# Low parts of weights by another VectorE instruction, and one in four of them by GpSimd in 56 units of the second table

## The reference

```
u   = peer_u[expert]                  # 128 rows per token, gathered
act = gelu(h . u)                     # one number per token and expert
y   = sum(gate * act * peer_v[expert])
out = layer_norm(alpha * h + y)
```

## Time and profile before

| what | us |
|---|---|
| median of three runs | 3760.6 |
| the profiled execution | 3774.7 |
| its span, first to last instruction | 3772.9 |
| first table, all 64 units, in the span | about 2265 to 3022 |
| second table, all 64 units, in the span | about 3022 to 3757 |

### The profile page before, as it was taken

How to read it: one execution, slowest core, us unless ns; L and a number is a source line. 1 busy time by engine, 2 the same in 40 slices (tenths; PEclk the granted TensorE clock), 3 DMA queues, 4 the chain that set the end, 5 groups by cost and what they waited for, 6 DMA issues and landing times.

```text
span 3772.9 us, 56020 instructions
## 1 busy us (share of the span) xinstructions
PE 3714.0 (98%) x22023; PEld 3316.4 (88%) x22023; DVE 2759.2 (73%) x3457; ACT 1404.1 (37%) x2037; POOL 1117.6 (30%) x579
## 2 busy tenths in 40 slices
PE   9999999999999999999999999999999999999998
PEld 8888888888987888888888899999999987878787
DVE  5655566565788765556556788899998877898888
ACT  5644444444335100000000144566664443434343
POOL 0000000001645433434444272332332223344342
PEclk9999999999999999999999999999999999999999
DMA  5345555554689999999999759999999999999996
GB/s 194 123 168 188 181 187 189 182 186 179 238 346 421 421 422 411 404 395 402 392 409 385 303 225 384 396 390 389 392 404 407 401 352 383 398 380 399 379 406 256
DMA packets 196692, 1232.58 MB, mean 327 GB/s; under 512 B 20336, under 2 KB 37312, under 8 KB 54976
## 3 DMA queue, kind: packets, MB, share of 16 engines
q1 hardware_dynamic: 110720, 656.51, 45.4%
q0 software_dynamic: 73728, 536.90, 34.8%
q10 hardware_dynamic: 12096, 37.23, 2.5%
HBM read 1193.34 MB, written 36.70 MB: 326 GB/s over the span
## 4 chain that ended last, share of the span: by engine, by line
PE 94%; DMA 3%; DVE 2%; issue 0%; ACT 0%; SPq 0%; DVEq 0%; ACTq 0%
PE dense_ps L1063 26%; PE dense_ps L1066 11%; PE dense_ps L1048 9%; PE dense_ps L1049 9%; PE dense_ps L1050 9%; PE dense_ps L1323 7%; PE dense_ps L1068 5%; PE score_ps L1323 4%; PE dense_ps L1096 3%; DMA wbuf<-in_peer_v_dram 2%; PE o_ps L1323 2%; PE oT_ps L1323 2%; PE dense_ps L1102 2%; PE score_ps L1285 2%; PE score_ps L1175 1%; PE oT_ps L1215 1%
## 5 line engine op out<-in xcount | busy, mean ns | idle before, releaser
L1448 DVE TENSOR_TENSOR w_three<-wbuf,w_three 128x1024 fp32r<-128x1024 f32 x792 | 961.4, 1222 | 457.4 <-ACT w_three L637 455.5
L637 ACT ACTIVATE w_three<-wbuf 128x1024 fp32r<-128x1024 f32 x848 | 890.8, 1059 | 1027.5 <-DMA wbuf<-in_peer_v_dram 235.7
L1048 PE MATMUL dense_ps<-act_two,w_three 128*128 128x256 f32 x2752 | 787.4, 286 | 3.9 <-DVE w_three L1448 3.7
L1049 PE MATMUL dense_ps<-act_two,w_three 128*128 128x256 f32 x2752 | 779.5, 283 | 0.0
L1050 PE MATMUL dense_ps<-act_two,w_three 128*128 128x256 f32 x2752 | 779.5, 283 | 0.0
L1063 PE MATMUL dense_ps<-xT,wbuf 128*128 128x256 f32 x3136 | 688.0, 380 | 0.0
L583 POOL DMA_INDIRECT row<-in_peer_v_dram,expert x203 | 424.5, 2091 | 855.1 <-DVE h L1400 820.1
L1063 PEld LDWEIGHTS dense_ps<-xT,wbuf 128*128 128x128 f32 x3136 | 593.9, 190 | 91.0 <-issue 11.4
L583 POOL DMA_INDIRECT row<-in_peer_u_dram,expert x256 | 449.3, 1755 | 586.8 <-DVE row L1395 526.2
L1395 DVE SCALAR_TENSOR_TENSOR row<-row,h 128x2048 f32<-128x2048 f32 x256 | 573.6, 2286 | 52.8 <-DMA row<-in_peer_u_dram,expert 52.7
L1048 PEld LDWEIGHTS dense_ps<-act_two,w_three 128*128 128x128 f32 x2752 | 529.1, 192 | 15.8 <-issue 11.8
(11 more groups left out here) (293 smaller groups left out, 4324.1 us busy)
## 6 DMA issues: line engine op xcount, KB each, us to landing
wbuf<-in_w_units_dram SPq DMA_DIRECT2D x456, 1024.0 KB
wbuf<-in_peer_v_dram SPq DMA_DIRECT2D x126, 1024.0 KB
gate_spill<-gbuf ACTq DMA_DIRECT2D x8, 2048.0 KB
e_gate<-gate_spill SPq DMA_DIRECT2D x32, 512.0 KB
act_spill<-stage ACTq DMA_DIRECT2D x60, 256.0 KB, 9.0
e_act<-act_spill SPq DMA_DIRECT2D x30, 512.0 KB
row<-in_peer_u_dram,expert POOLq DMA_INDIRECT x256
row<-in_peer_v_dram,expert POOLq DMA_INDIRECT x203, 10.9
```

What stands on the lines that cost most here:

```text
L637: act.activation(hi_of(n)[j // 2][:, j % 2, :], w_of(n)[j // 2][:, j % 2, :], ACT.Copy).then_inc(w_hi_ready, 1)
L1048: nc.tensor.matmul(out, w[0], x[0], start=opens, stop=False)
L1049: nc.tensor.matmul(out, w[0], x[1], start=False, stop=False)
L1448: V.tensor_tensor(lo_of(n)[j // 2][:, j % 2, :], w_of(n)[j // 2][:, j % 2, :], hi_of(n)[j // 2][:, j % 2, :].bitcast(F32), ALU.subtract).t ...
```

## The change

Three edits. (1) by_pool gives quarter 1 of units N_V+4 to N_V+59 (56 units) to GpSimd. (2) GpSimd's program for the second table goes unit by unit: for unit n it issues all gathers whose FREE is at most ROWS_TO[n-2], and then makes the low part of quarter 1 of unit n. (3) VectorE's low parts, in all units, are made by scalar_tensor_tensor (weight * 1.0 - high part) in place of tensor_tensor.

```diff
 def by_pool(n, j):
-    return U_PQ < n < UNITS or UNITS + U_PQ + PLAIN_Q <= n < N_U + 4
+    return U_PQ < n < UNITS or UNITS + U_PQ + PLAIN_Q <= n < N_U + 4 or j == 1 and N_V + 4 <= n < N_V + 60
...
-            def low(n):
-
-                for j in range(4):
+            def low(n, quarters=range(4)):
+
+                for j in quarters:
                     pool.wait_ge(w_hi_ready, HI[n, j])
...
-            for g in range(ROWS_TO[N_U + 1] + 3, LATE_ROWS):
-                gather(g)
-            pool.wait_ge(dense_ready, N_V)
-            for g in range(LATE_ROWS, ALL_ROWS):
+            g = ROWS_TO[N_U + 1] + 3
+            for n in range(N_V + 4, N_V + 62):
+                while g < ALL_ROWS and FREE[g] <= ROWS_TO[n - 2]:
+                    if g == LATE_ROWS:
+                        pool.wait_ge(dense_ready, N_V)
+                    gather(g)
+                    g += 1
+                if n < N_V + 60:
+                    low(n, (1,))
+            for g in range(g, ALL_ROWS):
                 gather(g)
...
                 dve.wait_ge(w_hi_ready, HI[n, j])
-                V.tensor_tensor(lo_of(n)[j // 2][:, j % 2, :], w_of(n)[j // 2][:, j % 2, :], hi_of(n)[j // 2][:, j % 2, :].bitcast(F32), ALU.subtract
-                                ).then_inc(lo_by_dve, 1)
+                V.scalar_tensor_tensor(out=lo_of(n)[j // 2][:, j % 2, :], in0=w_of(n)[j // 2][:, j % 2, :], scalar=1.0,
+                                       in1=hi_of(n)[j // 2][:, j % 2, :].bitcast(F32), op0=ALU.mult, op1=ALU.subtract
+                                       ).then_inc(lo_by_dve, 1)
```

## The result

The changed kernel takes 4045.8 us, the median of four runs (4035.7 to 4046.9), against 3760.0 before (four runs, 3755.3 to 3769.9): 1.076 times as long, with a 95% interval of 1.073 to 1.078. The profiled execution has a span of 4045.1 us, 272.2 more than before.

A forecast was written before the change was run, and what follows sets the result against it. TensorE, busy 98% of the span, was taken as the bound. Units of 17.5 us (15.2 plus 2.3 of clock) against 11.4, over 55 units, gave +336 on 3760.6: 4097 us, range 3950 to 4200.

The forecast's parts named there:

- the forecast's own case: Second table: GpSimd's late low part with the clock falling in each unit, 16.3 to 18.7 us per unit, 4030 to 4162; chance 0.67.
- The other form of the low part costs 0: VectorE's low parts in all units: scalar_tensor_tensor takes the same 1219 ns for 1024 elements as tensor_tensor, so 0 change.
- The row of 2283 ns: Trace row of VectorE's new instruction form at 2048 elements, against 2287 for tensor_tensor; taken as showing equal price.
- The chain of 9.2 us: Second table, from TensorE's third quarter through section n-2's last row, gather and GpSimd's low part: 9.2 us against 5.44 wanted.
- GpSimd and VectorE meet: GpSimd's low part and VectorE's next quarter 0 tie at 6.7 us; 14.6 or 15.8 us per unit, middle 15.2 taken.
- The clock: TensorE restarts at half clock after each unit's wait, losing 2.3 us per unit in quarters 1 and 2; bounds 0 and 2.9.
- 55 units: Units N_V+5 to N_V+59 are bound by the late low part, TensorE waiting for GpSimd some 55 times at 4 to 5 us.
- VectorE's low parts would stay at 1.22 us: In the profile after, VectorE's low parts keep 1.22 us; a change in their length would show the prediction wrong.
- The rival "faster": GpSimd's low part is in time and 64 us off VectorE win back waits: at most 35 us, 3726; chance 0.04.

The follow-up runs named there:

- 3833: The changed kernel, but the last gather before GpSimd's quarter 1 is one row earlier, so it waits for section n-2's last row but one; 3833.0 us, 1.0191.
- 3840: The changed kernel with quarter 3 of the same 56 units on GpSimd in place of quarter 1, same queue order and wait; 3839.7 us, 1.0215.
- 4271: The changed kernel with GpSimd's low part of the second table made twice, one after the other; 4271.5 us, 1.1362.
- the first experiment: The changed kernel, but GpSimd waits only for rows up to section n-3 before making quarter 1 of unit n; 3784.2 us, 1.0064.
- the ninth: The changed kernel with all low parts on VectorE; GpSimd instead subtracts 2 x 512 unused elements per unit, gathers a section earlier; 3787.5 us, 1.0077.
- the last experiment: The changed kernel with the same wait for section n-2's last row, but the gather that followed it issued behind GpSimd's low part; 3937.4 us, 1.0477.
- TensorE kept busy: The changed kernel with 12 further matmuls of 512 columns behind quarter 0 of each of the 56 units; 3969.8 us, 1.0552.

## Why the prediction was right, and where its terms were off

The time was forecast at 4097 and measured at 4046, inside the range and inside the forecast's own case; the change was forecast at +336 us and is +286. Point by point:

- *The other form of the low part costs 0.* Shown: 0.9998 with it alone. The row of 2283 ns was the right one to go by. The Trainium skill's rule on this instruction (Vector Engine (DVE) Microarchitecture Reference, "Points that are easy to get wrong") does not hold for these operands here: 1218 ns against 1219 at 1024 elements.
- *The chain of 9.2 us.* Shown: 9.16 us in the rows above, and by five runs that each change one thing in it: what it waits for (3784 and 3833), when its result is wanted (3840), one link more (4271), one link less (3937). The wait named was the one that ended last.
- *GpSimd and VectorE meet.* The prediction could not tell who comes first and took the middle, 15.2 us per unit. GpSimd gets in: VectorE's low part is recorded from 3512.56, GpSimd's from 3512.59, and it is VectorE's that takes 3.47 us. The chain is then 14.73 us; this term was 0.5 too high. The gather, of which the last 0.9 us run up to 3512.57, lies across VectorE's start and may be what holds it; that was not tried by itself.
- *The clock.* Forecast 2.3 us per unit, the mean of two restarts after 5.07 and 7.14 us. Measured 16.51 - 14.73 = 1.8, of which 0.1 is the mean wait of 3.67 us against the 3.55 of a plain unit: the clock itself is 1.7, as TensorE's 93 us of added busy time over 55 units are too. The waits are shorter than the two that the term was read from, and 9 of 55 units have no low clock at all. This term was 0.5 to 0.6 too high. The two terms together, about 1.0 us times 55, are the 51 us between forecast and result. That they came so close is in part luck: one was the middle of a tie, the other the mean of two restarts whose costs lay 1.25 us apart.
- *55 units.* 55 waits. They are 3.67 us on average where 4 to 5 was written, and so the stage is 1008 us for 1070, its clock 0.89 for 0.85 and its DMA share 0.73 for 0.65.
- *Failed: VectorE's low parts would stay at 1.22 us.* The prediction counted only GpSimd being held up by VectorE, and had named a change in the length of these low parts as a sign of its being wrong. In the changed kernel the median is 1.23 but the mean 1.81 us, as GpSimd holds one of them in most units. In the change this hides, for VectorE stands still for 321 us before its low parts anyway. With the chain removed some 26 us are left (3784), mostly nine waits for GpSimd low parts that were themselves held up.
- *The rival "faster"* rested on 64 us taken off VectorE. It did not come with GpSimd in time in 47 of 56 units either, in the first experiment: GpSimd lengthened VectorE's other instructions by 93 us and took 64 us off it, and TensorE's waits for VectorE went only from 12.9 to 10.7 us. In the ninth, 32 us were lost with no result of GpSimd's on the path.

None of the eleven versions is faster than the kernel before. What remained open: how far a GpSimd low part placed where VectorE runs no instruction with two inputs would help; it was not tried. Not every unit of this order can have such a place of 2.4 us, as VectorE stands still for only 1.7 us of a unit on average ((735 - 627) / 64).

## What to carry to other kernels

When work is moved to an engine with a long idle time, write down what stands in front of it in that engine's queue and what that waits for: here an idle engine delivered 3.7 us late on average in each of 55 units because of a gather's wait, a single gather ahead of the moved work cost 2 us per unit, and one section less of waiting gave back 262 of 286 us. Then look at whether the helper holds up the engine it is to relieve. A short wait of TensorE in every unit can cost more than its length: here 1.7 us per unit of lower clock came on top of 3.7 us of waiting.

## What was not expected of the hardware

- A GpSimd instruction with two SBUF inputs and VectorE's instructions with two SBUF inputs run one after the other, either way round: VectorE's of 1.22 us took up to 3.48 (in the changed kernel), GpSimd's of 2.35 up to 4.82 (in the first experiment). Work that nobody waits for slowed VectorE in the same way. The Trainium skill, SBUF — State Buffer, "Who interferes with whom", states that a VectorE instruction with two SBUF inputs contends with a GpSimd instruction that reads SBUF, and that the order of issue decides who waits. The timeline of the last experiment agrees, with VectorE's 2.48 us and GpSimd's 3.25. In the changed kernel the record alone would say otherwise, as VectorE's held instruction is recorded 0.03 us before GpSimd's; so starts this close do not tell who was first. The bill in the first experiment: with 56 GpSimd low parts VectorE's work took some 93 us longer.
- While VectorE went from one instruction to the next without a pause, GpSimd did not get in between at once, in the old form or in the new: gathers, 0.94 us when alone, took up to 8.4.
- The granted clock had time at 0.50 in 46 of 55 units of the changed kernel (waits of mostly 3.55 us), in 20 of 55 where the waits were mostly 2.57 us (the last experiment), and around 3 of 53 waits where they were mostly 0.87 us (TensorE kept busy). Two steps behind the same wait of 3.55 us differ, 14.7 against 16.3 us, so the length of one wait alone does not decide it.
